# One block per layer from output projection to down projection, with the norm between them in two token halves

## The chip, the cores and the metric

One NeuronCore of a Trainium2 chip runs the whole program. The metric is the device time of one execution in microseconds (us). TensorE (PE) multiplies matrices, VectorE (DVE) and ScalarE (ACT) work elementwise, GpSimd (POOL) does too, SyncE (SP) issues most transfers from HBM. PEld is TensorE's loading of weights.

## The reference

A decoder step over 560 tokens: 16 meta tokens with a 512-token prompt, and 8 sequences of 4 sample tokens. Two layers, width 1024. A layer is a mixer (mLSTM heads and forgetting attention in layer 0, retention and a gated linear recurrence in layer 1), an output projection, and a SwiGLU of width 2816; every sub-layer is normed on its way in and on its way out. What the change touches in the layer's second half is

```
h = h + rmsnorm(mix @ w_out, norm_g[layer, 1])
x = rmsnorm(h, norm_g[layer, 2])
ff = (silu(x @ wg) * (x @ wu)) @ wd
```

and, in the mixer of layer 0, the attention of the sample tokens over 1024 cached positions. These are read page by page: 8 pages of 128 positions for each of 8 sequences, found through a page table. All is float32.

## The kernel before

Activations lie in SBUF transposed, as 8 chunks of 128 features by 560 tokens. A product in float32 is made of three in a faster format (fp32r): weights and activations are each split into a high part (a copy by ScalarE) and a low part (a subtraction by VectorE), and PE computes high x high, high x low and low x high. One product instruction covers 128x128 weights and 280 tokens, so a chunk takes six: three products, two token halves (`HALF`), each half with its own PSUM bank.

`project` (L298) is one block: each engine has its instruction list, and a block ends when all engines have. Weights go through `ring`, two slots that SP refills (L210), and two split pieces `w_high`, `w_low` (L241, L245). PE takes a piece (L334) when VectorE has subtracted it and the bank is free. Results leave PSUM on VectorE (L385, L395, L398). In the gate/up projection ScalarE applies silu and GpSimd makes the hidden tile of 128 features and splits it, in three operations (L432 to L437).

`norm` (L517) is a block too. After the output projection it squares the output on three engines, PE sums the squares over features by a product with ones (plain float32, L504), ScalarE takes the root (L533), VectorE the reciprocal (L580), scales chunk by chunk and adds to `h` (L584, L588). ScalarE casts the new `h`, times the gain of the next norm, to the high part of the next input (L540) and squares it (L541), PE sums again, VectorE makes the low part (L592). Between its sums PE multiplies ones (`warm`, L451) with no use of the result. The second root (L357) is taken in the gate/up block, and the factor is applied to the outputs.

`close_layer` (L1763) strings four of these together after a fifth block (L1770) that splits the mixer's output, `xn`, into `mixed_high` and `mixed_low` and the first two weight pieces.

In the decode stage (block L1530) 16 steps go over K pages: a step takes one page index for four sequences. PE transposes four pages (L1563), VectorE and ScalarE copy them, PE computes scores (L1577). After step 10 the softmax of the first four sequences is turned (L1596) and multiplied with the V pages (L1611, the new tokens L1614); after step 15 that of the other four. SP issues K pages four at a time (L1281, `load_k`) and V pages eight at a time, one sequence each (L1287, `load_v`); before each call it reads page numbers into registers. V of sequences 4 to 7 goes into the buffers of the first four, so SP waits for `v_used`, which PE raises after the first products with V.

## Time and profile before

| what | us |
|---|---|
| median of three runs | 1977.45 (1973.34 to 1980.96) |
| the profiled execution | 1978.11 |
| its span, first to last instruction | 1976.6 |
| PE busy | 1748.8 |
| closing layer 0: block starts, PE starts, last product ends | 586.0, 598.1, 1099.6 |
| norm inside it, PE's last product before to first after | 649.2 to 679.8 |
| closing layer 1: PE starts, last product ends | 1439.4, 1940.6 |
| mean granted clock of TensorE | 0.921 |

Times in the rows are counted from the span's first instruction. An engine's idle time stands in brackets with what ended it; "PEq" is PE's own instruction queue, which at the edge of a block waits for the other engines. A granted clock of 1.00 is 2.4 GHz, 0.50 is 1.2 GHz.

### The profile page before, as it was taken

The numbers are of one execution on the slowest core, as the hardware profiler recorded it, in microseconds if no ns is written. First come the engines' busy times: TensorE is split into PE (matmuls) and PEld (weight loads), VectorE is DVE, ScalarE is ACT, GpSimd is POOL, SyncE is SP. The second block draws the span as 40 slices with busy tenths as digits, with TensorE's granted clock in tenths as the row PEclk, the third lists the DMA queues.
The fourth block names the chain that finished last, engine by engine and source line by source line (L and its number), as shares of the span: only waits on it lengthen the run. The fifth ranks groups of instructions, "written<-read, shape, count | busy, mean of one in ns | idle before, by whom it ended". The sixth has DMA issues, their size and how long they took to land. (4 is left out here: it accounts for less than half of the span.)

```text
span 1976.6 us, 31237 instructions
## 1 busy us (share of the span) xinstructions
PE 1748.8 (88%) x12539; PEld 1577.6 (80%) x12539; DVE 826.0 (42%) x1427; ACT 488.9 (25%) x634; POOL 297.2 (15%) x290
## 2 busy tenths in 40 slices
PE   5999897696758899999899899978488999998995
PEld 5999854555438699999899699955286999998995
DVE  3323645524333744444222633267637444442225
ACT  3111310141111433332111311133214333321111
POOL 1411001001000033333200000031300333332000
PEclk9999987597879999999899999988689999999998
DMA  4232210155652133333222122220121333332321
GB/s 124 90 91 70 65 26 0 48 171 170 219 185 77 33 85 85 85 85 93 77 79 70 42 68 85 96 68 0 50 65 43 84 85 84 85 88 73 82 56 45
DMA packets 225241, 159.60 MB, mean 81 GB/s; under 512 B 18041, under 2 KB 206437, under 8 KB 225048
## 3 DMA queue, kind: packets, MB, share of 16 engines
q1 hardware_dynamic: 220832, 156.40, 27.1%
q0 software_dynamic: 3280, 1.85, 0.4%
q8 instruction: 38, 0.62, 0.1%
q10 hardware_dynamic: 1064, 0.51, 0.1%
q14 instruction: 27, 0.22, 0.0%
HBM read 149.11 MB, written 9.88 MB: 80 GB/s over the span
## 5 line engine op out<-in xcount | busy, mean ns | idle before, releaser
L241 ACT CAST w_high<-ring 128x1024 fp32r<-128x1024 f32 (+1 forms) x188 | 207.1, 1104 | 914.1 <-PE psum L334 911.4
L334 PE MATMUL psum<-mixed_high,w_high 128*128 128x280 f32 x1664 | 352.0, 293 | 35.3 <-PEq L1770 29.0
L245 DVE TENSOR_TENSOR w_low<-ring,w_high 128x1024 fp32r<-128x1024 f32 (+1 forms) x188 | 289.6, 1544 | 155.7 <-ACT w_high L241 153.4
L334 PE MATMUL psum<-mixed_high,w_low 128*128 128x280 f32 x1664 | 353.9, 294 | 0.0
L334 PE MATMUL psum<-mixed_low,w_high 128*128 128x280 f32 x1664 | 350.9, 293 | 0.0
L334 PEld LDWEIGHTS psum<-mixed_high,w_high 128*128 128x128 f32 x1664 | 267.4, 190 | 36.9 <-issue 36.9
L334 PEld LDWEIGHTS psum<-mixed_high,w_low 128*128 128x128 f32 x1664 | 267.9, 191 | 0.0
L334 PEld LDWEIGHTS psum<-mixed_low,w_high 128*128 128x128 f32 x1664 | 265.3, 190 | 0.0
L334 PE MATMUL psum<-normed_high,w_high 128*128 128x280 f32 x832 | 175.3, 292 | 3.8 <-PEq L517 3.8
L334 PE MATMUL psum<-normed_high,w_low 128*128 128x280 f32 x832 | 175.7, 292 | 0.0
L334 PE MATMUL psum<-normed_low,w_high 128*128 128x280 f32 x832 | 174.7, 292 | 0.0
L334 PE MATMUL psum<-hidden_high,w_high 128*128 128x280 f32 x704 | 149.3, 294 | 15.7 <-PEq L298 15.7
L334 PE MATMUL psum<-hidden_low,w_high 128*128 128x280 f32 x704 | 149.5, 294 | 0.0
L334 PE MATMUL psum<-hidden_high,w_low 128*128 128x280 f32 x704 | 149.2, 294 | 0.0
L334 PEld LDWEIGHTS psum<-normed_high,w_high 128*128 128x128 f32 x832 | 132.7, 189 | 4.7 <-issue 4.7
L334 PEld LDWEIGHTS psum<-normed_high,w_low 128*128 128x128 f32 x832 | 133.1, 190 | 0.0
L334 PEld LDWEIGHTS psum<-normed_low,w_high 128*128 128x128 f32 x832 | 132.0, 189 | 0.0
L334 PEld LDWEIGHTS psum<-hidden_high,w_high 128*128 128x128 f32 x704 | 113.0, 191 | 16.1 <-issue 16.1
L432 POOL TENSOR_TENSOR silu<-silu,rstd 128x560 f32<-128x560 f32 x44 | 63.6, 1446 | 409.4 <-DVE silu L385 409.4
L395 DVE TENSOR_TENSOR projected<-psum,rstd 128x280 f32 (+1 forms) x104 | 41.9, 444 | 194.3 <-PE psum L334 194.2
L334 PEld LDWEIGHTS psum<-hidden_high,w_low 128*128 128x128 f32 x704 | 112.9, 191 | 0.0
L334 PEld LDWEIGHTS psum<-hidden_low,w_high 128*128 128x128 f32 x704 | 112.5, 190 | 0.0
(350 smaller groups left out, 1983.7 us busy)
## 6 DMA issues: line engine op xcount, KB each, us to landing
ring<-in_ffn_wg SPq DMA_DIRECT2D x44, 512.0 KB, 4.0
ring<-in_ffn_wu SPq DMA_DIRECT2D x44, 512.0 KB, 5.2
ring<-in_ffn_wd SPq DMA_DIRECT2D x16, 1408.0 KB, 6.9
projected<-in_cache_fox_k SPq DMA_DIRECT2D x64, 256.0 KB, 4.1
ring<-in_w_in_even SPq DMA_DIRECT2D x14, 1024.0 KB, 5.5
ring<-in_w_in_odd SPq DMA_DIRECT2D x12, 1024.0 KB, 5.1
v_pages<-in_cache_fox_v SPq DMA_DIRECT2D x32, 256.0 KB, 4.3
projected<-in_cache_fox_v SPq DMA_DIRECT2D x16, 256.0 KB, 4.0
```

The source lines that it names most:

```text
L241: nc.scalar.copy(part(high, p), raw(slot, p)).then_inc(high_done[p], 1)
L245: nc.vector.tensor_tensor(part(low, p), raw(slot, p), part(high, p).bitcast(F32), ALU.subtract).then_inc(low_done[p], 1)
L334: last = nc.tensor.matmul(banks[2 * tl + half][:, 0:HALF], w[:, k, :], m[:, half * HALF:(half + 1) * HALF], start=(kk == 0 and w is w_high ...
L395: c = nc.vector.tensor_tensor(out, banks[2 * tl + half][:, 0:HALF], rstd[:, cols_], ALU.mult)
L432: nc.gpsimd.tensor_tensor(silu[:, slot, :], silu[:, slot, :], rstd[:, :], ALU.mult)
```

## The change

`close_layer` becomes one block with semaphores of its own, which are cleared and given back after it. The same is done with those of the prompt attention and the decode stage (four closings, 38, 19, 33 and 33 semaphores). In the layer's block PE starts on the output projection when the first piece and the first chunk are split. ScalarE squares each output chunk as it leaves PSUM, and VectorE adds the squares up. The last two output tiles are computed by token halves, first half 0 of both; the norm then goes through half 0 and half 1 in turn. The first four gate/up tiles, whose weights are loaded ahead into a place of their own, are computed chunk by chunk as `h` comes out, with the sum of its squares. The hidden tiles lie in two arrays by token half. The `warm` products are gone here. SP's order of K and V pages in the decode stage changes too: V of sequence 2 goes in pairs between K pages, and V of the last four sequences page by page, four sequences at a time, with `v_step` telling PE of each page. "..." marks what is left out.

```diff
+        def new(name):
+            sems[name] = sems.get(name, 0) + 1
+            used.append(nc.alloc_semaphore(name=f"{name}_{sems[name]}"))
+            return used[-1]
+
+        def close():
+            nc.clear_and_free_semaphores(used)
+            nc.all_engine_barrier()
+        return new, close
...
+    def load_v_step(sp, pg):
+        _, pages = nc.values_load_multi_w_load_instructions(
+            step_ids[0:1, bass.ds(4 * (PAGES + pg), 4)], engines=[mybir.EngineType.SP], min_val=0, max_val=NPHYS - 1)
+        for slot, page in enumerate(pages):
+            sp.dma_start(vpage[slot][:, pg * 512:(pg + 1) * 512],
+                         cache_v[bass.ds(page, 1), :, :].rearrange("a t n -> (a t) n")).then_inc(v_step[pg], 16)
...
-            load_v(sp, 2)
             for s in range(2, STEPS):
+                if s < 6:
+                    load_v(sp, 2, 2 * (s - 2), 2)
                 load_k(sp, s)
-                if s >= STEPS - 4:
-                    if s == STEPS - 4:
-                        sp.wait_ge(v_used, 1)
-                    load_v(sp, 4 + s - (STEPS - 4))
+                if s == STEPS - 3:
+                    sp.wait_ge(v_used, 1)
+                if s >= STEPS - 3:
+                    load_v_step(sp, s - (STEPS - 3))
+            for pg in range(3, PAGES):
+                load_v_step(sp, pg)
...
-                for slot in range(4):
-                    pe.wait_ge(v_full[slot], 128 * (g + 1))
+                if g == 0:
+                    for slot in range(4):
+                        pe.wait_ge(v_full[slot], 128)
                 for pg in range(PAGES + 1):
+                    if g and pg < PAGES:
+                        pe.wait_ge(v_step[pg], 64)
...
+    close_decode_sems()
...
     def close_layer(layer, units, load_first=False):
...
-        high, low, _ = splitters(1, KC, pieces)
+        left.close()
...
             def _(sp):
                 if load_first:
                     prefetch(sp, units[0])
+                g, u_ = w_view(io["ffn_wg"][layer]), w_view(io["ffn_wu"][layer])
+                for u in range(2):
+                    dst = first_raw[:, u, :].rearrange("p (a k n) -> p a k n", a=2, k=KC)
+                    sp.dma_start(dst[:, 0], g[:, :, u * 128:(u + 1) * 128]).then_inc(first_full, 16)
+                    sp.dma_start(dst[:, 1], u_[:, :, u * 128:(u + 1) * 128]).then_inc(first_full, 16)
...
+                for u in (2, 3):
+                    when_split(u - 1)
+                    send(sp, units[0], u % 2, u)
+                for u in (2, 3):
+                    when_split(u + 1)
+                    send(sp, up[layer], u % 2, u)
...
+                for slot in range(2):
+                    when_split(31 + slot)
+                    if units[1] is not None:
+                        send(sp, units[1], slot, slot)
+
+            @block.tensor
+            def _(pe):
...
+                for n in range(6):
+                    p = n % 2
+                    pe.wait_ge(w_lo[p], n // 2 + 1)
+                    if n >= 2:
+                        pe.wait_ge(o_evac, 2 * n - 2)
+                    wh, wl = piece(p)
+                    for k in range(KC):
+                        if n == 0:
+                            pe.wait_ge(mix_h, k + 1)
+                            pe.wait_ge(mix_l, k + 1)
+                        last = both(p, wh[:, k], wl[:, k], x_of(x_h, k), x_of(x_l, k), k == 0, k == KC - 1)
+                    last.then_inc(used[p], 1)
...
+                for n in (6, 7):
+                    pe.wait_ge(w_lo[n % 2], 4)
+                    half_tile(n, 0).then_inc(half_done, 1)
+                pe.wait_ge(o_acc, 5)
+                mm(banks[1][:, 0:HALF], ones[:, :], acc[:, HALVES[0]], start=True, stop=False)
+                pe.wait_ge(o_sq, 13)
+                mm(banks[1][:, 0:HALF], ones[:, :], sq[6][:, HALVES[0]], start=False, stop=False)
+                half_tile(6, 1).then_inc(used[0], 1)
+                pe.wait_ge(o_sq, 14)
+                mm(banks[1][:, 0:HALF], ones[:, :], sq[7][:, HALVES[0]], start=False, stop=True).then_inc(o_sum, 1)
+                half_tile(7, 1).then_inc(used[1], 1)
...
+                def first_products(k, a, tiles):
+                    pe.wait_ge(xh_done, KC * a + k + 1)
+                    for t in tiles:
+                        bank = banks[2 * t + a][:, 0:HALF]
+                        if k == 0 and a == 0:
+                            pe.wait_ge(first_lo, t + 1)
+                        mm(bank, fw[t][0][:, k], x_h[:, k, HALVES[a]], start=(k == 0), stop=False)
+                        mm(bank, fw[t][1][:, k], x_h[:, k, HALVES[a]], start=False, stop=False)
+                    pe.wait_ge(xl_done, KC * a + k + 1)
+                    for t in tiles:
+                        last = mm(banks[2 * t + a][:, 0:HALF], fw[t][0][:, k], x_l[:, k, HALVES[a]], start=False,
...
+                for k in range(KC):
+                    first_products(k, 0, range(4))
+                    if k == 1:
+                        pe.wait_ge(o_sq, 16)
+                        for i, src in enumerate((acc, sq[6], sq[7])):
+                            last = mm(banks[3][:, 0:HALF], ones[:, :], src[:, HALVES[1]], start=(i == 0), stop=(i == 2))
+                        last.then_inc(o_sum, 1)
+                        pe.wait_ge(o_evac_b, 2)
+                    if k:
+                        h_square(k - 1, 0)
+                h_square(KC - 1, 0)
+                for k in range(KC):
+                    first_products(k, 1, range(3))
+                    if k == 2:
+                        pe.wait_ge(h_root, 1)
+                        h_square(0, 1)
+                        h_square(1, 1)
+                    if k >= 2:
+                        h_square(k, 1)
+                pe.wait_ge(h_root, 2)
+                for k in range(KC):
+                    first_products(k, 1, (3,))
...
+                with pe.Fori(0, 4) as i:
+                    for slot in range(2):
+                        for p in range(2):
+                            pe.wait_ge(w_lo[p], i * 2 + (25 + slot))
+                            if p == 0:
+                                pe.wait_ge(tile_evac[2 * slot], i + 11)
+                            for s in range(2):
+                                pe.wait_ge(hid_done[s], 10 + p)
...
             @block.scalar
...
+                out_high(0)
                 for k in range(KC):
-                    nc.scalar.copy(x[0][:, k, :], xn[:, k, :]).then_inc(s_mh, 1)
-                    if k == 5:
+                    nc.scalar.copy(x_h[:, k, :], mixed[:, k, :]).then_inc(mix_h, 1)
+                    if k == 3:
+                        out_high(1)
...
+                act.wait_ge(o_sum, 1)
+                nc.scalar.activation(rpost[:, HALVES[0]], banks[1][:, 0:HALF], ACT.Sqrt, bias=eps[:, 0:1],
+                                     scale=1.0 / D).then_inc(o_root, 1)
+                for n in (6, 7):
+                    act.wait_ge(used[n % 2], 4)
+                    bank = banks[2 * (n - 4) + 1]
+                    square(n, 1, bank[:, 0:HALF])
+                    nc.scalar.copy(o[:, n, HALVES[1]], bank[:, 0:HALF]).then_inc(o_evac_b, 1)
...
+                for a in range(2):
+                    for k in range(KC):
+                        act.wait_ge(h_done, KC * a + k + 1)
+                        nc.scalar.mul(x_h[:, k, HALVES[a]], h[:, k, HALVES[a]], gain(layer, 2, k)).then_inc(xh_done, 1)
+                        nc.scalar.activation(sq[k][:, HALVES[a]], h[:, k, HALVES[a]], ACT.Square).then_inc(h_sq, 1)
+                        if a == 0 and k == 2:
+                            act.wait_ge(o_sum, 2)
+                            nc.scalar.activation(rpost[:, HALVES[1]], banks[3][:, 0:HALF], ACT.Sqrt, bias=eps[:, 0:1],
+                                                 scale=1.0 / D).then_inc(o_root, 1)
+                        if a == 1 and k == 2:
+                            h_root_of(0)
+                        if a == 1 and k in (3, 5):
+                            p = (k - 3) // 2
...
             @block.vector
...
+                out_low(0)
+                for k in range(KC):
+                    dve.wait_ge(mix_h, k + 1)
+                    v.tensor_tensor(x_l[:, k, :], mixed[:, k, :], x_h[:, k, :].bitcast(F32), ALU.subtract).then_inc(mix_l, 1)
+                    if k == 5:
+                        out_low(1)
...
+                for n in (6, 7):
+                    dve.wait_ge(half_done, n - 5)
+                    v.tensor_copy(o[:, n, HALVES[0]], banks[2 * (n - 4)][:, 0:HALF]).then_inc(o_evac, 1)
...
+                for a in range(2):
+                    c = HALVES[a]
+                    dve.wait_ge(o_root, a + 1)
+                    v.reciprocal(rpost[:, c], rpost[:, c])
+                    if a:
+                        dve.wait_ge(o_evac_b, 2)
+                    v.drain()
+                    for step in range(KC + 2):
+                        k = step
+                        if k < KC:
+                            v.scalar_tensor_tensor(out=o[:, k, c], in0=o[:, k, c], scalar=gain(layer, 1, k), in1=rpost[:, c],
+                                                   op0=ALU.mult, op1=ALU.mult).then_inc(y_done, 1)
+                        k = step - 1
+                        if 0 <= k < KC:
...
+                            v.tensor_tensor(h[:, k, c], h[:, k, c], o[:, k, c], ALU.add).then_inc(h_done, 1)
...
+                            dve.wait_ge(xh_done, KC * a + k + 1)
+                            v.scalar_tensor_tensor(out=x_l[:, k, c], in0=h[:, k, c], scalar=gain(layer, 2, k),
+                                                   in1=x_h[:, k, c].bitcast(F32), op0=ALU.mult,
+                                                   op1=ALU.subtract).then_inc(xl_done, 1)
...
-                for k in (1, 4, 7):
-                    split_x(pool, nc.gpsimd, k)
-        left.close()
-        left = ExitStack()
-        project(units[0], 1, 2, KC, chunk(x), o, 0, pieces, then=up[layer], split=True)
-        norm(o, (layer, 1), (layer, 2), squares, x, splitters(2, KC, pieces, True))
-        project(up[layer], 2, FC // 2, KC, chunk(x), hid, 0, pieces, then=down[layer],
-                silu=place(silu, "silu", [128, 2, T]), normed=True, following=(1, FC, False))
-        project(down[layer], 1, 4, FC, chunk(hid), ffn_out, 0, pieces, then=units[1], split=True)
+                        pool.wait_ge(tile_evac[2 * slot + 1], i + 1)
+                        g.tensor_tensor(silu[:, slot, :], silu[:, slot, :], rstd[:, :], ALU.mult)
+                        g.drain()
+                        hh, hl = ([t[:, bass.ds(i * 2 + slot, 1), :].rearrange("p a t -> p (a t)") for t in a]
+                                  for a in (hid_h, hid_l))
+                        for a in range(2):
+                            g.tensor_copy(hh[a], silu[:, slot, HALVES[a]])
+                        g.drain()
+                        for a in range(2):
+                            last = g.tensor_tensor(hl[a], silu[:, slot, HALVES[a]], hh[a].bitcast(F32), ALU.subtract)
+                        last.then_inc(hid_done[slot], 1)
+        close_sems()
+        ffn_out = out
```

## Rows read from the trace of the kernel before

**Rows 1.** The page: engine, busy us (share of the span) xinstructions.
```profile
PE 1748.8 (88%) x12539; PEld 1577.6 (80%) x12539; DVE 826.0 (42%) x1427; ACT 488.9 (25%) x634; POOL 297.2 (15%) x290
```

**Rows 2.** List of waits: who waited for whom, us, times, longest us.
```profile
PE psum L334 <- PEq L1770: 29.0, 2, 15.1
...
PE psum L1563 <- DMA projected<-in_cache_fox_k: 23.8, 6, 9.6
```

**Rows 3.** Stretches: busy (x) of PE PEld DVE ACT POOL, clock, DMA, GB/s.
```profile
598.00:650.00 52.00, 51.08 (x384) 50.86 (x384) 13.73 (x22) 6.30 (x6) 0.00 (x0) 0.97 0.27 81
649.00:680.00 31.00, 24.73 (x75) 13.11 (x75) 29.43 (x37) 17.73 (x28) 2.69 (x2) 1.00 0.00 1
680.00:954.00 274.00, 273.19 (x2112) 272.97 (x2111) 112.24 (x133) 85.73 (x87) 87.14 (x63) 0.99 0.32 87
...
680.00:684.00 4.00, 4.00 (x21) 4.00 (x21) 3.61 (x2) 1.58 (x2) 0.00 (x0) 0.59 0.79 220
961.00:966.00 5.00, 4.96 (x21) 4.97 (x22) 0.00 (x0) 0.00 (x0) 0.00 (x0) 0.50 0.85 240
```

**Rows 4.** Timeline, norm of layer 0: start, us, what [idle before].
```profile
654.55 4.04 PE L504 MATMUL psum<-squares,ones 128*128 128x280 f32 x16 [0.48 <-DVE squares L573]
...
658.16 0.97 ACT L533 ACTIVATE rstd<-psum,eps 128x280 f32<-128x280 f32 x2 [2.04 <-PE psum L504]
...
658.69 3.66 DVE L580 RECIPROCAL rstd<-rstd 128x280 f32<-128x280 f32 x2
```

**Rows 5.** Timeline, start of closing layer 0, all engines.
```profile
591.67 1.04 ACT L241 CAST w_high<-ring 128x1024 fp32r<-128x1024 f32 x1 [2.15 <-DMA ring<-in_w_out_even]
...
593.31 0.74 DVE L1786 TENSOR_TENSOR mixed_low<-mixed,mixed_high 128x560 fp32r<-128x560 f32 x1 [1.50 <-ACT mixed_high L1779]
...
598.14 0.83 PE L334 MATMUL psum<-mixed_high,w_high 128*128 128x280 f32 x2 [13.88 <-PEq L1770]
```

**Rows 6.** Timeline, start of closing layer 1, all engines.
```profile
1428.92 3.46 ACT L1779 CAST mixed_high<-mixed 128x560 fp32r<-128x560 f32 x6 [4.04 <-PEq L461]
...
1436.41 2.35 DVE L245 TENSOR_TENSOR w_low<-ring,w_high 128x1024 fp32r<-128x1024 f32 x2
...
1439.41 0.83 PE L334 MATMUL psum<-mixed_high,w_high 128*128 128x280 f32 x2 [15.13 <-PEq L1770]
```

**Rows 7.** Groups by line and form: xcount | busy us, mean ns | idle.
```profile
L398 DVE COPY projected_out<-psum 128x280 f32<-128x280 f32 x32 | 12.9, 445 | 74.8 <-PE psum L334 74.8
```

**Rows 8.** Timeline, from gate/up to down in layer 0.
```profile
954.11 2.68 POOL L432 TENSOR_TENSOR silu<-silu,rstd 128x560 f32<-128x560 f32 x1 [7.76 <-DVE silu L385]
...
961.03 0.83 PE L334 MATMUL psum<-hidden_high,w_high 128*128 128x280 f32 x2 [7.84 <-PEq L298]
```

**Rows 9.** Timeline of SP's transfers, decode stage.
```profile
471.14 40.63 SPq L1281 DMA_DIRECT2D projected<-in_cache_fox_k  x44
527.56 4.29 SPq L1287 DMA_DIRECT2D projected<-in_cache_fox_v  x8
533.41 1.89 SPq L1281 DMA_DIRECT2D projected<-in_cache_fox_k  x4
...
554.23 1.88 SPq L1281 DMA_DIRECT2D projected<-in_cache_fox_k  x4
```

**Rows 10.** Timeline of PE, decode stage.
```profile
523.71 1.06 PE L1614 MATMUL psum<-token_major_v,projected 32*32 32x512 f32 x8
...
571.95 1.06 PE L1611 MATMUL psum<-projected 128*32 128x512 f32 x1 [0.89 <-DVE projected L1696]
...
581.67 1.06 PE L1614 MATMUL psum<-token_major_v,projected 32*32 32x512 f32 x8
```

**Rows 11.** The page: DMA issues, xcount, KB each, us to landing.
```profile
v_pages<-in_cache_fox_v SPq DMA_DIRECT2D x32, 256.0 KB, 4.3
```

**Rows 12.** Line L298 (block edges), instructions: ns min/median/max.
```profile
L298 POOLq EVENT_SEMAPHORE  x18: 17/17/17, 140.3 to 1941.6; - x18
...
L298 PEldq DRAIN  x9: 2260/2268/2270, 134.9 to 1938.3; - x9
```

More of the change, by code:

```diff
@@ L1776, in _, with high @@
             @block.scalar
             def _(act):
[L1778 to L1786 removed]
+                def high(dst, src, p):
+                    nc.scalar.copy(dst, src).then_inc(w_hi[p], 1)
@@ new lines, in _ @@
+                for n in range(6):
+                    p = n % 2
+                    act.wait_ge(used[p], n // 2 + 1)
+                    out_high(n + 2)
+                    for a in range(2):
+                        act.wait_ge(o_evac, 2 * n + a + 1)
+                        square(n, a, o[:, n, HALVES[a]])
+                    if 1 <= n < 5:
+                        t = n - 1
+                        act.wait_ge(first_full, 64)
+                        nc.scalar.copy(f_h[:, t, :], first_raw[:, t // 2, (t % 2) * 1024:(t % 2 + 1) * 1024]).then_inc(first_hi, 1)
@@ L1788, in _, with low @@
+                with act.Fori(0, 3) as i:
+                    for slot in range(2):
+                        down_turn(i, slot)
+                down_turn(3, 0)
             @block.vector
             def _(dve):
-                for k in (0, 2, 3, 5, 6):
-                    split_x(dve, nc.vector, k)
-                for p in range(2):
-                    low(dve, 0, 0, p)
+                v = nc.vector
+                def low(dst, src, high_, p, count):
+                    dve.wait_ge(w_hi[p], count)
+                    v.tensor_tensor(dst, src, high_.bitcast(F32), ALU.subtract).then_inc(w_lo[p], 1)
@@ new lines, in up_low, with up_evac @@
+                def up_low(slot, p, count):
+                    low(w_l[:, p, 0:1024], up_raw(slot, p), w_h[:, p, 0:1024], p, count)
+                def up_evac(i, q):
+                    slot, p = q // 2, q % 2
+                    dve.wait_ge(used[p], i * 2 + (5 + slot))
+                    if p:
+                        dve.wait_ge(silu_act[slot], i + 1)
+                    elif not (isinstance(i, int) and i == 0):
+                        dve.wait_ge(hid_done[slot], i)
+                    for a in range(2):
+                        c = HALVES[a]
+                        last = v.tensor_tensor(silu[:, slot, c], silu[:, slot, c] if p else rstd[:, c],
+                                               banks[2 * q + a][:, 0:HALF], ALU.mult)
+                    last.then_inc(tile_evac[q], 1)
@@ new lines, in up_turn @@
+                def up_turn(i, last):
+                    for q in range(4):
+                        up_evac(i, q)
+                        p = q % 2
+                        slot = 1 - q // 2
+                        if last and q >= 2:
+                            low(w_l[:, p, :], down_raw(slot, p), w_h[:, p, :], p, 25)
+                        else:
+                            up_low(slot, p, i * 2 + (4 + q // 2))
+                up_low(0, 0, 5)
+                for a in range(2):
+                    dve.wait_ge(h_root, a + 1)
+                    v.reciprocal(rstd[:, HALVES[a]], rstd[:, HALVES[a]])
@@ new lines, in _, with down_turn @@
+                v.drain()
+                for q in range(4):
+                    up_evac(0, q)
+                    if q == 0:
+                        up_low(0, 1, 5)
+                with dve.Fori(1, 10) as i:
+                    up_turn(i, False)
+                up_turn(10, True)
+                def down_turn(i, slot, more):
+                    for p in range(2):
+                        if p:
+                            dve.wait_ge(used[1], i * 2 + (27 + slot))
+                            for a in range(2):
+                                o_ = out[:, bass.ds(i * 2 + slot, 1), HALVES[a]].rearrange("p a t -> p (a t)")
+                                last = v.tensor_copy(o_, banks[4 * slot + a][:, 0:HALF])
+                            last.then_inc(tile_evac[2 * slot], 1)
+                        if more:
+                            low(w_l[:, p, :], down_raw(1 - slot, p), w_h[:, p, :], p, i * 2 + (26 + slot))
```

226 lines of the change are left out of this document (192 added, 34 removed).

## The prediction

> **What bounds the kernel now.** I read the page's busy shares first: TensorE (PE) works 88% of the span [rows 1], more than twice as long as any other engine, so a change is worth what it takes out of PE's idle time or out of PE's work done at half clock. The list of waits says where PE idles: at the edges of blocks and on K pages of the decode stage [rows 2]; the two edges of layer closing (L1770) alone are 29.0 us. The table by stretch then gives the pace inside a stage [rows 3]: the gate/up block is 2112 matmuls in 273.2 us, nearly all at full clock. Its first 4 us were granted 0.59, which loses 4 x 0.41 = 1.6, so a matmul of 280 columns costs (273.2 - 1.6) / 2112 = 128.6 ns when PE is fed. Between output projection and gate/up lie 649.23 to 679.77, 30.5 us in which PE does only sums of squares and filler products. There the chain is serial: sums, root, reciprocal, 8 chunks, then a new block. The timeline shows its links [rows 4].
>
> **Part 1: start of the layer's block.** Before, PE waits until all eight chunks and both weight pieces are split and a block has ended; after, its first product needs one piece and one chunk. Layer 0 [rows 5]: the block begins at 586.0; ScalarE takes the weights at 591.67. After: ScalarE copies the piece (1.04), VectorE subtracts (1.2, half of 2.35 [rows 6]) and makes one chunk's low part (0.74), so PE starts 5.7 + 1.04 + 1.2 + 0.74 = 8.7 us into the block, where it took 598.14 - 586.0 = 12.1: gain 3.4. Layer 1 has its weights already [rows 6]: 1.04 + 1.2 + 0.74 = 3.0 against 1439.41 - 1428.9 = 10.5: gain 7.5. VectorE then delivers a chunk every 0.65 to 0.74 us and PE eats one in 6 x 128.6 = 0.77 (1.4 at half clock), so PE stays fed. GpSimd's three subtractions move to VectorE; VectorE's lone one is 0.74. The four loads of first gate/up weights are issued behind the output weights on SP and ahead of its waits for splits; their user is two pieces later, over 12 us. ScalarE now waits for the output weights ahead of the casts of the chunks; that is the 5.7 above. Sum: 10.9.
>
> **Part 2: the norm in two halves.** Before, from the end of tile 5 to the end of the first four gate/up tiles: 96 matmuls 12.3 + 30.5 + 192 matmuls 24.7 + 1.6 for half clock = 69.1 us. After, PE has the same 288 matmuls, 37.0, plus 22 products with ones. These are plain f32 (two records each): 8 of them took 4.04 us [rows 4], 0.505 each, 11.1 together. Cover now matters. After half 0's last sum PE has 24 matmuls (3.1 us); beside it run the root 0.49, the reciprocal of 280 columns 1.9 (half of 3.66), two scalings and one addition 1.3, a cast 0.45 (estimates from the 445 below): 4.2 us and hand-offs of 0.3. ScalarE must first square and copy tile 7's second half, some 0.9 after PE ends it, which is no later. PE idles about 1.4. Then a chunk of half 0 is 12 matmuls and one sum, 2.05 us, against VectorE's three operations. A half-width one is not in the before norm; the nearest is the 280-column copy, 445 ns [rows 7] (a lower bound is half of the 560-column subtraction's 0.74 [rows 5], an upper the whole), so 1.33 per chunk, at most 2.2: hidden, or 0.15 short a chunk. ScalarE waits at chunk 2 of half 1 for half 0's sums; behind it stand the casts of chunks 3 to 7, which PE wants only after three more chunks. Half 1's root of h needs its own sums; PE waits a root's 0.5 there, then has 3.1 us of tile 3 against root, reciprocal and evacuation, 3.3. Idle 2.2 in all: 37.0 + 11.1 + 2.2 = 50.3. Gain 18.8 a layer, 37.6 for two. Bounds: idle of 0 (41) to 10 us a layer (22).
>
> **Part 3: gate/up to down.** PE idles 7.84 while GpSimd finishes the last hidden tile [rows 8] and the block ends, then runs at half clock in layer 0 (0.50 all through 961 to 966 [rows 3]; I take 5.6 us, cost 2.8) and, I estimate from the other edges, 1.6 in layer 1. After, the first down piece reads only hidden tiles 0 to 10: 66 x 0.1286 = 8.5 us of cover, against less than the 7.84 that VectorE's evacuation, GpSimd's three operations and the edge took together. GpSimd's two passes become four of half width, hidden as long as they add under 1.4. Gain 7.84 x 2 + 2.8 + 1.6 = 20.1; bounds 12 to 20.
>
> **Part 4: decode loads, which the short title leaves out.** SP issues all K and V pages, and every step begins with reading page numbers into registers. Today K of step 13 queues behind V of a whole sequence: PE ends at 524.77, SP sends eight V pages only then, PE idles 9.64 for K [rows 2, 9, 10]. After, SP waits once, after K(13), then sends V and K in fours; behind that wait stand all of V and K(14), as they did before, but no longer K(13). One such step costs 533.41 - 531.85 = 1.56 for the numbers and 1.89 for issuing, 3.45. From 524.8: V0, K14, V1, K15 end at 538.6, where K15 ended at 556.1: 17.5 earlier. The chain behind K15 (transposes, softmax, values starting 571.95) moves to 554.5. V2 to V7 need 6 x 3.5 more, to 559.6, plus 4.3 to land [rows 11]: 564; PE's values take 9.7, of which the last page must be there after 8.5, at 563.0. So loads end last by a us: 564 + 1.2 + 1.1 = 566.3 against 582.7, gain 16.4. Ahead of that, V of sequence 2 no longer holds K(2) until 471.14, but the same issuing is spread over four steps, with three more register reads; K(12) gains 0 to 4, I take 2. Sum 18; bounds 12 to 20.
>
> **Part 5: what is added.** Four closings clear 123 semaphores (38, 19, 33, 33) and make all engines meet; nothing covers them. No row shows a clear. Below: GpSimd's semaphore instructions take 17 ns [rows 12], 2.1 us for all, and an edge with nothing to drain some 0.3 (an estimate from two such instructions and the hand-off to five queues), together 3.3. Above: each closing also pays a drain like PE's 2.27, 12 us. I take 6, plus 2 for PE falling to half clock in the longer gaps, since no filler runs there: 8.
>
> **Sum.** 10.9 + 37.6 + 20.1 + 18 - 8 = 78.6. The profiled execution took 1978.1 (1976.6 and 1.5 around it), 0.03% above the median of three runs, so the same sum holds for that: 1978 - 79 = 1899 us. Own range 1887 to 1910.
>
> **Rivals.**
> 1. *VectorE bounds the norm.* 24 operations per norm become 48 of half width. From rows, 2 x 445 - 740 = 150 ns more for each pair, 3.6 us per norm, hidden behind 2.05 us per chunk as long as VectorE and ScalarE overlap. If ScalarE's two operations and VectorE's three run one after the other with PE, each of 16 half-chunks costs PE 1.3 more, 42 us over both layers: 1941. For it: in the norm before, VectorE is busy 29.4 of 31 us [rows 3]. Against: PE's 50 us of work now stand beside the same operations, and ScalarE's 17.7 run beside VectorE's. Chance 0.09. The Trainium skill speaks for it: "VectorE: DVE Perf Modes", section "The TRN2 errata — SBUF-src ops pay a fixed extra latency per instruction", wants tiles of 512 elements or more since each instruction pays a fixed cost. This trace agrees that halving costs (740 ns for 560, 445 for 280 columns), and the sum holds that cost already; the rule decides only where VectorE is the bound.
> 2. *Decode gains nothing*, since V now lands later than softmax ends: K earlier, values stretched over V's landing. For it: DMA is busy there; against: four pages take 2.1 of 3.45 us to issue and landed evenly. 1899 + 16 = 1915. Chance 0.10.
> 3. *Closings are dear*: the GpSimd clear works semaphore by semaphore with its own drains, 5 us more each: 1919. Chance 0.10.
> 4. *Slower: the clock stays down.* If PE's gap at the first half's root lets the clock fall and the stage, with its waits inside, never gets it back until the gate/up loop, 48 us of PE work a layer take 96. Two layers: 1899 + 96 = 1995. It decides from 40 us a layer on. For it: behind the idle edge before 680 it is 0.59 over 4 us; against: the shorter edge at 649 left it at 1.00 over the whole norm [rows 3], and PE is over 90% busy in the new stage. Chance 0.03.
> 5. *Hidden tiles still late*, part 3 gives only the clock: 1914. Chance 0.06.
>
> **Numbers.** Forecast 0.62: 1899. From 1883 (closings 3.3, decode 20.4, no idle: 4.7 + 2.4 + 4.4 less, and the 4 by which the lowest of three runs lies under the median) to 1922 (closings at 12 with decode at 12 is 1911; case 3 is 1919) the range takes in cases 2, 3 and 5. Outside stay case 1, case 4 and 0.08 of the tails: 0.80 inside. A measurement of this kernel can tell about 0.5%, 10 us, from no change. Only case 4 (0.03) ends above that; 0.02 I leave for several losses at once between 1968 and 1988; the rest, 0.95, is faster.
>
> **What would show it.** PE's first product about 8.7 and 3 us into the layer blocks; no PE gap over 2.5 us from there to the last down product; PE 50 us from tile 5's end to the gate/up loop; no gap of 9 us before K(13); values ending near 566 minus what came before. Wrong would be: gaps at every chunk of the norm, granted clock 0.5 inside the layer block, or closings over 3 us.

## The result, and the profile after

The changed kernel takes 1896.22 us (median of 4 runs, 1894.63 to 1897.34), the kernel before 1978.55 (4 runs, 1973.34 to 1980.96): ratio 0.9587, 95% interval 0.9565 to 0.9608, so 4% faster. In a second set of five runs it took 1895.99. The forecast was 1899 (1883 to 1922). The profiled execution after took 1895.25, with a span of 1893.7.

The page of the kernel after, PE's row, beside [rows 1]:

```profile
PE 1712.2 (90%) x12483; PEld 1557.9 (82%) x12483; DVE 820.0 (43%) x1475; ACT 450.0 (24%) x656; POOL 292.3 (15%) x368
```

PE is busy 36.6 us less. More than half of that is filler that is gone, the `warm` products, which kept PE busy while it waited in the norm. Their group before, from 649 to 680 in layer 0:

```profile
L451 PE MATMUL psum<-ones 128*128 128x512 f32 x24 | 10.7, 596 | 1.2 <-PEq L298 1.2
```

Another part is work that is no longer done at a lower clock (0.59 and 0.50 in two stretches of [rows 3]). The rest of the 82 us was idle time. The list of waits of PE after (over the whole span, then over layer 0's block alone from its first product), beside [rows 2]:

```profile
PE psum L1883 <- DVE mixed_low L2118: 19.6, 2, 11.8
...
PE psum L1593 <- DMA projected<-in_cache_fox_k: 9.3, 11, 1.9
...
PE psum L1644 <- DMA ring<-in_cache_fox_v: 4.8, 2, 2.8
```
```profile
PE psum L1883 <- DVE mixed_low L2118: 11.8, 1, 11.8
PE psum L1937 <- ACT mixed_high L2052: 1.4, 1, 1.4
PE psum L1937 <- ACT rstd L2046: 0.6, 1, 0.6
```

The two starts of a closing layer fell from 29.0 to 19.6 us, the waits for K from 23.8 to 9.3; waits for V (L1644) are new, 4.8. From its first product in layer 0 to its last, 472 us later, PE idles in two places only, 1.4 and 0.6 us.

By stretch, after (columns as in [rows 3]): the norm between the projections, the gate/up loop with the start of the down projection, the rest of the latter, the middle of the program that the change leaves alone, the whole of layer 1; and then the end of decode with the start of layer 0.

```profile
636.90:672.00 35.10, 34.49 (x234) 32.38 (x235) 26.43 (x51) 17.51 (x38) 0.00 (x0) 1.00 0.00 1
672.00:930.00 258.00, 258.00 (x2008) 258.00 (x2008) 107.28 (x128) 56.11 (x62) 97.43 (x110) 1.00 0.33 90
930.00:1055.00 125.00, 124.78 (x968) 124.56 (x966) 27.15 (x29) 17.80 (x13) 0.00 (x0) 1.00 0.27 75
1055.00:1375.00 320.00, 274.98 (x1649) 231.37 (x1650) 173.69 (x374) 84.62 (x117) 38.32 (x33) 0.91 0.19 60
...
1384.40:1857.00 472.60, 470.62 (x3596) 467.78 (x3596) 191.16 (x247) 112.05 (x150) 97.46 (x110) 0.99 0.28 77
```
```profile
553.00:561.00 8.00, 5.21 (x52) 1.49 (x48) 0.00 (x0) 0.00 (x0) 0.00 (x0) 0.95 0.91 304
561.00:568.00 7.00, 4.97 (x24) 0.40 (x16) 0.00 (x0) 0.00 (x0) 0.00 (x0) 0.50 0.23 78
568.00:571.00 3.00, 1.66 (x8) 0.71 (x4) 1.16 (x4) 0.00 (x0) 0.00 (x0) 0.50 0.00 0
571.00:582.00 11.00, 0.00 (x0) 0.00 (x0) 2.66 (x8) 2.77 (x5) 0.00 (x0) 0.50 0.74 220
582.00:588.00 6.00, 5.67 (x26) 5.70 (x27) 5.88 (x9) 3.70 (x6) 0.00 (x0) 0.54 1.21 291
588.00:620.00 32.00, 32.00 (x253) 32.00 (x252) 17.31 (x23) 12.32 (x19) 0.00 (x0) 1.00 0.32 100
```

PE is nearly full at full clock (2.4 GHz) from 588 to the layer's end. At half clock (1.2 GHz) it runs from 561 on, behind its waits for V, until some us into the output projection.

Cut at PE's first and last products, and set beside the terms of the prediction's sum:

| piece | before | after | gain | forecast |
|---|---|---|---|---|
| decode, end of prompt attention to PE's last product | 123.0 | 109.4 | 13.6 | 18 |
| idle to layer 0's first product | 13.9 | 11.8 | 2.1 | 3.4 |
| layer 0, first to last product | 501.4 | 472.4 | 29.0 | 29.4 |
| middle, with the edges of its own | 324.8 | 321.8 | 3.0 | 0 |
| idle to layer 1's first product | 15.1 | 7.8 | 7.4 | 7.5 |
| layer 1, first to last product | 501.2 | 472.6 | 28.5 | 28.2 |
| idle behind layer 1 | 1.2 | 1.9 | -0.7 | 0 |
| closings, as a term of their own | | | in the pieces | -8 |
| sum | | | 82.9 | 78.6 |

### The profile page after: what moved, and what is told of

Read it like the earlier page. It is cut to its first block and busy times, and to the rows that moved or that the text cites. A ratio compares the mean times of both kernels' runs of the same rounds, so it can differ in the third digit from the quotient of the medians.

```text
span 1893.7 us, 31309 instructions
## 1 busy us (share of the span) xinstructions
PE 1712.2 (90%) x12483; PEld 1557.9 (82%) x12483; DVE 820.0 (43%) x1475; ACT 450.0 (24%) x656; POOL 292.3 (15%) x368
## 3 DMA queue, kind: packets, MB, share of 16 engines
q1 hardware_dynamic: 220832, 156.40, 28.3%
## 5 line engine op out<-in xcount | busy, mean ns | idle before, releaser
L1883 PE MATMUL psum<-mixed_high,w_high 128*128 128x280 f32 x1472 | 310.5, 292 | 19.6 <-DVE mixed_low L2118 19.6
L1883 PE MATMUL psum<-mixed_high,w_low 128*128 128x280 f32 x1472 | 312.1, 293 | 0.0
L1883 PE MATMUL psum<-mixed_low,w_high 128*128 128x280 f32 x1472 | 309.7, 292 | 0.0
L2003 ACT CAST w_high<-ring 128x1024 fp32r<-128x1024 f32 (+1 forms) x128 | 144.5, 1129 | 664.3 <-PE psum L1883 631.1
L2110 DVE TENSOR_TENSOR w_low<-ring,w_high 128x1024 fp32r<-128x1024 f32 (+1 forms) x128 | 212.6, 1661 | 142.6 <-ACT w_high L2003 142.6
L255 ACT CAST w_high<-ring 128x1024 fp32r<-128x1024 f32 x52 | 54.4, 1050 | 253.6 <-PE psum L348 253.0
L1883 PE MATMUL psum<-hidden_low_b,w_high 128*128 128x280 f32 x352 | 102.8, 292 | 0.0
L1883 PE MATMUL psum<-hidden_high_b,w_high 128*128 128x280 f32 x352 | 102.8, 292 | 0.0
L1883 PE MATMUL psum<-hidden_high_a,w_high 128*128 128x280 f32 x352 | 102.7, 292 | 0.0
L1883 PE MATMUL psum<-hidden_high_b,w_low 128*128 128x280 f32 x352 | 102.4, 291 | 0.0
```

The costliest lines, as they stand in the source:

```text
L255: nc.scalar.copy(part(high, p), raw(slot, p)).then_inc(high_done[p], 1)
L1883: done = mm(banks[2 * tl + a][:, 0:HALF], w, m[a], start=first and s == 0, stop=last and s == 2)
L2003: nc.scalar.copy(dst, src).then_inc(w_hi[p], 1)
L2110: v.tensor_tensor(dst, src, high_.bitcast(F32), ALU.subtract).then_inc(w_lo[p], 1)
```

## The experiments

Ratios are to the kernel before, run on the same chip beside each. Where an experiment is compared with the changed kernel, that is 1896.2. The kernel before took 1978.59, 1976.33 and 1975.17 in the three sets of experiments, so a comparison across sets is good to some 3 us.

**Decode order alone**: the kernel before with the new order of V and K loads (with it come PE's wait for each V page and the two closings of that stage).

```diff
-            load_v(sp, 2)
             for s in range(2, STEPS):
+                if s < 6:
+                    load_v(sp, 2, 2 * (s - 2), 2)
                 load_k(sp, s)
-                if s >= STEPS - 4:
-                    if s == STEPS - 4:
-                        sp.wait_ge(v_used, 1)
-                    load_v(sp, 4 + s - (STEPS - 4))
+                if s == STEPS - 3:
+                    sp.wait_ge(v_used, 1)
+                if s >= STEPS - 3:
+                    load_v_step(sp, s - (STEPS - 3))
+            for pg in range(3, PAGES):
+                load_v_step(sp, pg)
```

> The kernel before with the decode stage's changes alone: the new order of K and V pages, the wait for each page of V, and the two closings of that stage. Theory (the load order is worth what the decode stage got shorter, 123.0 to 109.4 us from the end of the attention before it to PE's last product, less some 0.6 for the second closing): 13 us faster, 1965 us. Rival (PE would have waited for V anyway, and the 13.6 us came from the clock's phase): under 5 us, 1974 or more.

1966.21 us, ratio 0.9938 (0.9918 to 0.9957): 12.4 less. PE's K waits in this kernel:

```profile
PE psum L1593 <- DMA projected<-in_cache_fox_k: 7.9, 10, 1.8
```

The order is worth its share by itself; the longest K wait is 1.8 instead of 9.6.

**The layers alone**: the changed kernel with the old decode order (the diff above, reversed).

> The changed kernel with the old order of K and V pages in the decode stage; everything else as changed. Theory (terms add up): the changed kernel's 1896 plus 14, 1910 us, so 68 us for the two layer blocks. Rival (the two halves help each other, for example since a decode stage that ends earlier finds the clock in another state): 1904 or less, or 1916 or more.

1908.77 us, ratio 0.9645 (0.9623 to 0.9667): 69.8 less than before. The two add up to 82.2, the whole change is 82.3: the parts do not share a gain.

**The down projection waits for all hidden tiles.**

```diff
-                                pe.wait_ge(hid_done[s], 10 + p)
+                                pe.wait_ge(hid_done[s], 11)
```

> The changed kernel, except that already the first piece of the down projection waits for all hidden tiles, as a block's end made it do before. Theory (the gap of 7.84 us was the last hidden tile, which 8.5 us of products now cover): PE idles about 7 us per layer there and then runs 1.6 to 2.8 at half clock's cost, 17 to 20 us slower than the changed kernel, 1914. Rival (the gap was the end and start of a block; the last hidden tile is quick): under 5 us slower, below 1901.

1916.38 us, ratio 0.968 (0.9657 to 0.9704), 20 more than with the split wait. PE at the start of the down projection of layer 0, here and then in the changed kernel:

```profile
930.47 0.57 PE L1883 MATMUL psum<-hidden_high_a,w_high 128*128 128x280 f32 x1 [6.26 <-POOL hidden_low_b L2234]
```
```profile
918.48 0.29 PE L1883 MATMUL psum<-hidden_high_a,w_high 128*128 128x280 f32 x1
```

The wait comes back, and a product takes 0.57 instead of 0.29 behind it: half clock. Layer 0 is 480.0 us long here, 7.6 more, layer 1 480.9, 8.3 more: 16 of the 20. Another 5.5 lie in the decode stage, which this edit does not touch and which took 114.9 in this execution.

**The first gate/up products wait for the whole first half** (and the second half's squares are summed ahead of them).

```diff
+                pe.wait_ge(o_sq, 16)
+                for i, src in enumerate((acc, sq[6], sq[7])):
+                    last = mm(banks[3][:, 0:HALF], ones[:, :], src[:, HALVES[1]], start=(i == 0), stop=(i == 2))
+                last.then_inc(o_sum, 1)
+                pe.wait_ge(o_evac_b, 2)
+                pe.wait_ge(xl_done, KC)
                 for k in range(KC):
                     first_products(k, 0, range(4))
-                    if k == 1:
...
```

> The changed kernel, except that PE starts on the first gate/up products of token half 0 only when all eight chunks of that half are normed and split; the sums for half 1 are moved ahead of them. Theory (chunk-by-chunk products cover VectorE's chain, 8 chunks of 1.29 us): PE idles 8 to 9 us more per layer, and the clock falls for some 3.4 us, 9 to 12 us per layer, 18 to 24 in all, 1916 us. Rival (VectorE's chain binds either way, PE only waits at other places): under 6 us slower, below 1902.

1915.94 us, ratio 0.9687 (0.9663 to 0.971), 19.7 more than the changed kernel; 16.1 of them lie in the two layers (480.0 and 481.1 us from first to last product). PE's first such product in layer 0:

```profile
647.89 0.57 PE L1937 MATMUL psum<-mixed_high,first_w_high 128*128 128x280 f32 x1 [7.37 <-issue]
```

"issue" means that the profile shows no releaser for this wait; by the diff it is the last chunk's `xl_done`, the signal that its low part is made, and VectorE's last low part of this half ends at 647.79, 0.1 us earlier. Behind the wait a product takes 0.57 us: half clock. So a good part of the norm's gain, 8 us a layer, hangs on PE following VectorE chunk by chunk.

**The output projection waits for all eight chunks.**

```diff
-                            pe.wait_ge(mix_h, k + 1)
-                            pe.wait_ge(mix_l, k + 1)
+                            pe.wait_ge(mix_h, KC)
+                            pe.wait_ge(mix_l, KC)
```

> The output projection's first tile waits for the high and low parts of all eight chunks, as before the change; everything else as after. Theory (the early start by chunks is worth what VectorE's splitting takes beyond the first chunk): the last chunk's low part comes 7 x 0.65 to 0.74 us = 4.6 to 5.2 us behind the first one's, and PE's start in each layer moves by that, less what it has to wait within the first tile today (nothing): about 5 us a layer, 10 in all, 1906 us against the changed kernel's 1896. Rival (the start waits for the weights, not for the chunks): under 1.5 us a layer, at most 1899.

1909.0 us, ratio 0.9665 (0.9639 to 0.969): 13 more, where 10 were expected. PE's first products of the two layers:

```profile
588.43 0.80 PE L1883 MATMUL psum<-mixed_high,w_high 128*128 128x280 f32 x2 [16.55 <-DVE mixed_low L2118]
```
```profile
1398.74 0.81 PE L1883 MATMUL psum<-mixed_high,w_high 128*128 128x280 f32 x2 [13.46 <-DVE mixed_low L2118]
```

4.8 and 5.7 us more idle time, 10.5 in both: the mechanism holds. In the profiled executions the rest lies in pieces that this edit does not touch, the middle above all (322.7 here, 320.0 in the changed kernel).

**VectorE does more in the norm.**

```diff
                         k = step - 2
                         if 0 <= k < KC:
+                            v.scalar_tensor_tensor(out=o[:, k, c], in0=o[:, k, c], scalar=gain(layer, 1, k), in1=rpost[:, c],
+                                                   op0=ALU.mult, op1=ALU.mult)
```

> VectorE does one more half-width operation (a product of three, some 0.50 us) for each of the 16 half chunks of each layer's norm, into a place that nobody reads again; outputs stay as they were. Theory (PE's 2.05 us a chunk covers VectorE's 1.28): with 1.28 + 0.42 = 1.70 a chunk VectorE is still covered; only what stands ahead of the first product of each half grows, by one such operation, 4 x 0.4 = 1.6 us in all: 1896 to 1898. Rival (VectorE sets the norm's pace): 32 x 0.42 = 13.4 us more, 1909.

1894.75 us, ratio 0.9593 (0.9572 to 0.9615): nothing. The same 14 us of the norm, in the changed kernel and with the additional operations:

```profile
650.00:664.00 14.00, 14.00 (x96) 13.21 (x96) 11.94 (x24) 8.62 (x19) 0.00 (x0) 1.00 0.00 1
```
```profile
650.00:664.00 14.00, 14.00 (x96) 13.17 (x95) 13.36 (x28) 7.50 (x16) 0.00 (x0) 1.00 0.00 0
```

VectorE is busy 13.4 of 14 us there and costs nothing; PE is as full as before.

**V pages 5 to 7 on GpSimd's queue.**

```diff
-            for pg in range(3, PAGES):
+            for pg in range(3, 5):
                 load_v_step(sp, pg)
...
+            pool.wait_ge(v_used, 1)
+            for pg in range(5, PAGES):
+                load_v_step(pool, pg, mybir.EngineType.Pool)
```

> In the decode stage V pages 5 to 7 of the second group are issued on GpSimd's queue, behind the same wait for V's buffer, while SP keeps pages 0 to 4. Theory (the values wait for SP's reading and issuing, about 3.5 us a page, not for the DMA engines): V is all there some 8 us earlier, PE's two waits of 2.79 and 2.03 us on V pages go, and half clock behind them shortens: 4 to 6 us off, 1890 to 1892. Rival (the DMA engines or K's transfers are the limit, and pages that come earlier hold up K of steps 14 and 15): no gain, or 1 to 4 us slower, 1896 to 1900.

1896.36 us, ratio 0.9598 (0.9577 to 0.962): nothing; the theory falls. (The profiled execution was the longest of six, 1906.4, so its trace is read for the transfers alone.) Use of the DMA engines in 40 slices of the decode's end (525 to 565 us after, 530 to 565 here), and the time from issue to landing, in the changed kernel and then with two queues:

```profile
DMA  0479968789699989797899769898898978997610
...
projected<-in_cache_fox_k SPq DMA_DIRECT2D x8, 256.0 KB, 3.7
```
```profile
DMA  0003979989999999999999999999999999950000
...
v_pages<-in_cache_fox_v SPq DMA_DIRECT2D x10, 256.0 KB, 7.5
projected<-in_cache_fox_k SPq DMA_DIRECT2D x8, 256.0 KB, 9.9
```

V's waits are gone from this trace, but the DMA engines are full without a break, and K of steps 14 and 15, issued among V's pages, lands 9.9 us after its issue instead of 3.7. From 537 to 553 the transfers ran at 284 to 310 GB/s with one queue and at 384 to 385 with two. What V gains K loses, as far as this one trace shows.

**GpSimd adds the squares of h in pairs**, so PE has half as many products with ones.

```diff
+                for a in range(2):
+                    c = HALVES[a]
+                    for k in range(1, KC, 2):
+                        pool.wait_ge(h_sq, KC * a + k + 1)
+                        g.tensor_tensor(sq[k][:, c], sq[k - 1][:, c], sq[k][:, c], ALU.add).then_inc(h_pair, 1)
```

> GpSimd adds the squares of h in pairs of chunks before PE sums them, so that PE runs 8 instead of 16 plain f32 products with ones in each layer's norm. Theory (PE is the bound there and each such product costs its 0.505 us): 16 x 0.505 = 8.1 us less over both layers, minus some 0.8 us a layer at the end of each norm, where PE waits for the last pair: 1889.5. Rival (GpSimd's work slows VectorE in the same stage, or PE waits for pairs): no gain or slower, 1896 or more.

1891.01 us (1887.87 to 1896.01), ratio 0.958 (0.9555 to 0.9605): 5.2 less than the changed kernel, 0.3%, which is less than the measurement can tell for sure. The stretch of the norm from the first gate/up product on is 31.2 us in both layers instead of 34.8, so 7.2 were saved in the trace. PE waits for no pair. The rival's slowing of VectorE is there, but covered. VectorE's operations beside GpSimd's addition in this kernel (two answers, VectorE and then GpSimd):

```profile
640.73 1.05 DVE L2153 SCALAR_TENSOR_TENSOR projected_out<-projected_out,cols,post_rstd 128x280 f32<-128x280 f32 x1
641.70 0.44 DVE L2158 TENSOR_TENSOR h<-h,projected_out 128x280 f32<-128x280 f32 x1
...
642.49 0.50 DVE L2153 SCALAR_TENSOR_TENSOR projected_out<-projected_out,cols,post_rstd 128x280 f32<-128x280 f32 x1
...
659.18 1.82 DVE L2112 TENSOR_TENSOR w_low<-ring,w_high 128x1024 fp32r<-128x1024 f32 x1
```
```profile
640.68 0.79 POOL L2229 TENSOR_TENSOR squares<-squares,squares 128x280 f32<-128x280 f32 x1 [4.12 <-ACT squares L2055]
643.11 0.89 POOL L2229 TENSOR_TENSOR squares<-squares,squares 128x280 f32<-128x280 f32 x1 [1.64 <-ACT squares L2055]
...
659.12 0.80 POOL L2229 TENSOR_TENSOR squares<-squares,squares 128x280 f32<-128x280 f32 x1 [1.64 <-ACT squares L2055]
```

The same scaled operation (L2153) takes 1.05 us while GpSimd works and 0.50 when it does not. The subtraction of a weight piece (L2112) takes 1.82 beside GpSimd; in the changed kernel it takes 1.22 where GpSimd is idle:

```profile
616.86 1.22 DVE L2110 TENSOR_TENSOR w_low<-ring,w_high 128x1024 fp32r<-128x1024 f32 x1 [0.35 <-ACT w_high L2003]
```

**Squares and ones in fp32r.**

```diff
-        sq = [at("squares", col, [128, T]) for col in (24848, 25408, 25968, 26912, 27472, 28032, 33072, 33632)]
-        acc = at("square_sum", 34192, [128, T])
+        sq = [at("squares", col, [128, T], F32R) for col in (24848, 25408, 25968, 26912, 27472, 28032, 33072, 33632)]
+        acc = at("square_sum", 34192, [128, T], F32R)
+        ones_r = at("ones_r", 26528, [128, 128], F32R)
...
-                    last = mm(banks[7][:, 0:HALF], ones[:, :], sq[k][:, HALVES[a]], start=(k == 0), stop=(k == KC - 1))
+                    last = mm(banks[7][:, 0:HALF], ones_r[:, :], sq[k][:, HALVES[a]], start=(k == 0), stop=(k == KC - 1))
```

> The squares, their running sum and the ones that they are multiplied with are held in fp32r, the type of all other matmuls of the layer, so each square is rounded a little before it is summed (the mean of 1024 of them is used). Theory (PE is the bound in the norm, and a plain f32 product costs 0.505 us where an fp32r one costs 0.129): 22 x 0.376 = 8.3 us less a layer, 16.5 in all, 1880 us; in trace, no new idle time of PE. Rival (with 1.67 instead of 2.05 us a chunk, VectorE's 1.28 and ScalarE's two operations set the pace, or PE waits for the square before): a third of it or less, 1891 or more.

1880.4 us (1878.12 to 1884.24), ratio 0.9522 (0.9504 to 0.954); the changed kernel beside it 1895.99, so 15.6 less. PE's waits between the projections of layer 0, as in the changed kernel:

```profile
PE psum L1938 <- ACT mixed_high L2054: 1.4, 1, 1.4
PE psum L1938 <- ACT rstd L2048: 0.6, 1, 0.6
```

No new wait: PE was the bound there. This beats both kernels.

**The same with VectorE's additional operations.**

> The same with one more VectorE operation of half width per half chunk, into a place that nobody reads again. Theory (the cover that made this operation free, 1896.2 to 1894.8, was PE's work): VectorE takes 1.70 us a half chunk, 27 us for all 16, where PE has 13.4 + 10.3 = 24; PE waits 3 to 4 us a layer, 6 to 8 us more than without the operation, near 1887. Rival (VectorE's run ahead still hides it): less than 3 us more.

1891.63 us (1885.4 to 1898.48), ratio 0.9578 (0.9555 to 0.96). The trace has the stretch of the norm at 31.5 us against 28.3 without the operations, 3.2 a layer, 6.5 in all, as the theory says; the profiled execution took 7.3 more (1885.4 against 1878.1), the median 11.2 more. The scatter of these five runs, 13 us, stays unexplained. PE's waits in layer 0's norm here:

```profile
PE psum L1938 <- ACT mixed_high L2054: 2.2, 2, 1.4
...
PE psum L1942 <- DVE mixed_low L2164: 0.4, 2, 0.2
```

The list has only 1.2 us of the 3.2 as waits; shorter ones are probably hidden in products whose ends are modelled. With 8 us less of PE work a layer, the operation that was free (1894.75 against 1896.2) has a price.

**The changed kernel once more.**

> The changed kernel once more, beside these two on one chip: 1896 us, as before; within 3 us.

1895.99 us (1894.06 to 1901.63).

## Why the prediction was right

**Part 1, starts.** Layer 1 starts 7.4 us earlier (7.5 forecast), layer 0 2.1 (3.4): a closing of 0.7 us stands ahead of its block, and ScalarE could take the output weights 6.3 us into the block, not 5.7. PE started 9.4 us into the block, not 8.7. The later start belongs to this one execution: in the second profiled one of the same kernel the weights could be taken at 5.4 and PE started 8.5 us into the block, after 11.0 us of idle time and not 11.8:

```profile
584.00 0.81 PE L1883 MATMUL psum<-mixed_high,w_high 128*128 128x280 f32 x2 [10.97 <-DVE mixed_low L2118]
```

So the forecast of the start held (in layer 1, 3.1 us into the block where 3.0 was forecast), and what it left out is the closing. With the wait for all chunks put back, 4.8 and 5.7 of idle time returned: that the early start hangs on the chunks is shown. That one weight piece is enough for it was not tested by itself.

**Part 2, norm.** The step "PE 50 us from tile 5's end to the gate/up loop" (50.3) measured 50.06 in both layers. Its idle places of 1.4 and 0.5 measured as below; the third, 0.2 at tile 3, is not among PE's waits. (Two slips of the sum change nothing: with no idle time the two layers gain 42.0, not 41, and half of 3.66 is 1.83, not 1.9, though the reciprocal of 280 columns did take 1.90.)

```profile
636.93 0.40 PE L1937 MATMUL psum<-mixed_high,first_w_high 128*128 128x280 f32 x1 [1.38 <-ACT mixed_high L2052]
```
```profile
668.35 0.40 PE L1937 MATMUL psum<-mixed_high,first_w_high 128*128 128x280 f32 x1 [0.58 <-ACT rstd L2046]
```

VectorE's half-width operations, all three kinds (groups by line and form), lie between the bounds given, 370 and 740 ns:

```profile
L2160 DVE SCALAR_TENSOR_TENSOR mixed_low<-h,cols,mixed_high 128x280 fp32r<-128x280 f32 x32 | 16.2, 505 | 8.4 <-ACT mixed_high L2052 8.4
L2151 DVE SCALAR_TENSOR_TENSOR projected_out<-projected_out,cols,post_rstd 128x280 f32<-128x280 f32 x32 | 15.8, 504 | 0.3
L2156 DVE TENSOR_TENSOR h<-h,projected_out 128x280 f32<-128x280 f32 x32 | 14.2, 442 | 0.0
```

They overlap a little, so a chunk takes 1.20 us (those of L2151 start at 636.23, 637.43 and 638.63); 1.33 was forecast. Rival 1, VectorE as the bound, is refuted by the run with more VectorE work, and its condition is seen in the fp32r pair: it decides once PE's work a chunk falls below VectorE's. The Trainium skill's rule against small tiles ("VectorE: DVE Perf Modes", section "The TRN2 errata — SBUF-src ops pay a fixed extra latency per instruction") is true to this trace in the price (792 ns for a scaled operation of 560 columns, 505 for one of 280), but not in the verdict here: the price fell into PE's cover. One size was a little off: 22 products with ones at 0.505. The fp32r run saved 15.5 us in the two layers' traces, 0.35 a product; with the 0.129 that is left that makes 0.48.

**Part 3, gate/up to down.** PE goes from the last gate/up to the first down product without a gap (the row of 918.48 above) and stays at full clock. The layers gained 29.0 and 28.5 where parts 2 and 3 make 29.4 and 28.2. Waiting for all hidden tiles costs 16 of it back inside the layers.

**Part 4, decode.** This term was too large, 13.6 for 18. SP's transfers after, beside [rows 9]:

```profile
525.82 0.34 SPq L1312 DMA_DIRECT2D projected<-in_cache_fox_v  x1
...
529.27 2.43 SPq L1297 DMA_DIRECT2D projected<-in_cache_fox_k  x4
...
536.68 1.88 SPq L1297 DMA_DIRECT2D projected<-in_cache_fox_k  x4
...
559.17 0.33 SPq L1312 DMA_DIRECT2D ring<-in_cache_fox_v  x1
```

K(15) ends at 538.56 (538.6 forecast), the last V page is issued at 559.5 (559.6). But these are the times before the 2 us for K(12) are taken off: they did not come. And PE at the last two V pages, then at the new tokens (the first two rows are the first products of either page):

```profile
560.78 1.06 PE L1644 MATMUL psum<-projected 128*32 128x512 f32 x1 [2.79 <-DMA ring<-in_cache_fox_v]
...
564.75 1.06 PE L1644 MATMUL psum<-projected 128*32 128x512 f32 x1 [2.03 <-DMA ring<-in_cache_fox_v]
...
566.61 1.93 PE L1647 MATMUL psum<-token_major_v,projected 32*32 32x512 f32 x8
```

The last values end at 568.5, not at 566.3. The wait for the last page ends at 564.75 and not at 564; behind it PE is at half clock (0.50 from 561 on), so the page's products take 1.9 where the sum had 1.2, and those of the new tokens 1.93 where [rows 10] had 1.06. These 2.2 and the 2 for K(12) make 4.2 of the 4.4. That V is bound by SP's issuing, as the sum had it, is true only up to the DMA engines' limit close above: a second queue gained nothing.

**Part 5, closings.** The term that was most off: 6 us, and 2 for the clock. A closing is one clear of all its semaphores and a meeting of the engines (instructions of their lines, ns min/median/max, first and last start):

```profile
L127 POOLq EVENT_SEMAPHORE_RANGE_CLEAR  x4: 137/220/240, 462.0 to 1858.2; - x4
```
```profile
L128 POOLq EVENT_SEMAPHORE  x8: 17/17/17, 462.2 to 1858.7; - x8
```

From GpSimd's drain ahead of the clear to the last engine's release it is 0.55 to 0.72 us each, 2.6 for all four, below the lower bound of 3.3: the clear is one instruction for a range, not one a semaphore. Rival 3 is refuted. The idle edges behind the layers grew by just 0.6 and 0.7. Of the 2 us for the clock about 1 is seen: the stretch of 6 us at PE's start in layer 0 was granted 0.54 after (582 to 588) and 0.72 before (598 to 604), a loss of 2.8 against 1.7; in layer 1 the first 6.6 us were granted 0.60 and 0.62.

**The sum** came out 4.3 low: decode 4.4 and the starts 1.4 too much, the closings 6.7 too dear by what shows at the edges behind the layers (the other two lie in the decode stage and in the start of layer 0), and 3.6 in the middle between the layers, whose code is the same (the rest is in the layers and in rounding). That middle takes 320.0 to 323.6 us in the executions profiled here, and 320.0 and 322.7 in the two of the changed kernel alone. So most of the 3.6 is scatter and no gain of the change, and the sum's closeness is part luck.

**Rivals 2, 4 and 5** did not come: decode alone gained 12.4; the clock stayed at 1.00 from 588 to the end of the layer, past the 1.4 us gap; the hidden tiles are in time.

## What to carry to other kernels

A stage whose chain is serial (sums, root, reciprocal, chunks) was shortened here by giving the bounding engine other work in the same block, half the data at a time, with a wait for each chunk; the added instructions of the other engine were free as long as the bounding engine's work a chunk was the longer, and that is a sum to make first. When it is done, what is left is the bounding engine's own work: here 22 plain float32 products a layer at 0.48 us each, which fp32r brought to 0.129 for a further 15.6 us, with squares that are rounded a little before they are summed. For transfers that come late, see first whether the DMA engines are already near full before giving them a second queue.

## What the runs showed of the hardware

- Clearing a range of semaphores is one instruction: 0.14 us for 19 of them, 0.22 for 33, 0.24 for 38.
- VectorE operations with two inputs in SBUF took longer while GpSimd was adding: a scaled one of 280 columns 1.05 us (0.50 otherwise), a subtraction of 1024 columns 1.82 (1.22 otherwise). Over the norm the mean of the operation that makes the low part rose from 506 to 670 ns. The Trainium skill ("GPSIMD Engine Reference", section "1. Specifications") names contention between the two for instructions with two SBUF inputs; the trace agrees for both kinds. Ten additions of 280 columns kept their 438 ns, but GpSimd's addition overlapped each by less than 0.25 us, so they tell nothing against it. The reciprocal, with one input, kept its 1.90 us beside a whole addition of GpSimd.
- Two queues moved the V and K pages at some 385 GB/s once the DMA engines were full, one queue at 284 to 310 in the same stretch; over the windows shown the means are 302 and 264. No time was saved.
